# Where the query weights wait, and in what order the matrix engine takes expert rows and queries

## The reference

```python
def peer_ffn(h, w_q, sub_keys, expert_u, expert_v):     # 8 heads, 2 x 128 sub-keys, top 16
    q = einsum('cd,de->ce', xc, w_q)                     # (C, 8, 2, 128): 8 heads, 256 wide each
    s = einsum('chpk,pnk->chpn', q, sub_keys)
    sv, si = top_k(s, 16)                                # per half
    cand = sv[:, :, 0, :, None] + sv[:, :, 1, None, :]   # 256 candidates
    top_v, top_pos = top_k(cand, 16)
    gate = softmax(top_v)
    u = expert_u[eid]; act = gelu(einsum('cd,chkd->chk', xc, u))
    y = einsum('chk,chkd->cd', gate * act, expert_v[eid])
x = x + g2 * y
return rmsnorm(x, final_g)
```

## Time and profile before

| | |
|---|---|
| median of 3 executions | 1353.65 us (1345.6, 1353.65, 1353.81) |
| the profiled execution | 1349.08 us, of which the traced span 1347.3 us |
| mean granted PE clock | 0.939 |
| busy: PE, DVE, POOL, ACT | 85%, 67%, 33%, 19% |
| DMA | 412.99 MB, mean 307 GB/s |

### The profile page before, as it was taken

One profiled execution on the slowest core, in us unless ns is written; L12 is line 12 of the kernel. 1 busy time (PEld: TensorE's weight loads), 2 busy tenths in 40 slices (PEclk: granted clock), 3 DMA queues, 4 the chain that ended last, 5 costly groups with the idle time before them and its releaser, 6 DMA issues.

```text
span 1347.3 us, 13673 instructions
## 1 busy us (share of the span) xinstructions
PE 1147.1 (85%) x4566; PEld 756.0 (56%) x4566; DVE 903.4 (67%) x2164; ACT 258.0 (19%) x434; POOL 438.3 (33%) x351
## 2 busy tenths in 40 slices
PE   4899988986999996897999997778778787878876
PEld 3788877846999994864665653333323233323322
DVE  6453437535788886442577888696877869778565
ACT  2114022005333333432320101001010100101001
POOL 0000000012455541310134465444444444545430
PEclk9889999997999997898999999889999888998898
DMA  9546455543677664221399999999999999999992
GB/s 384 199 188 264 174 218 219 218 188 125 250 299 285 283 286 185 94 94 36 153 422 421 420 419 421 422 420 422 421 420 422 421 421 422 421 422 421 421 421 120
DMA packets 57220, 412.99 MB, mean 307 GB/s; under 512 B 6480, under 2 KB 6480, under 8 KB 7120
## 3 DMA queue, kind: packets, MB, share of 16 engines
q0 software_dynamic: 42912, 311.97, 56.3%
q1 hardware_dynamic: 14256, 100.37, 19.1%
HBM read 411.26 MB, written 1.05 MB: 306 GB/s over the span
## 4 chain that ended last, share of the span: by engine, by line
PE 54%; DMA 27%; DVE 12%; issue 4%; ACT 2%; POOL 1%; SPq 0%; DVEq 0%; ACTq 0%
PE ps L420 13%; PE ps L908 10%; DMA areaB<-in_experts,idx 7%; DMA gate_area<-in_experts,idx 7%; PE ps L433 6%; PE ps L435 6%; PE ps L434 5%; DMA ring<-in_experts,idx 4%; DMA mod_ring<-in_experts,idx 3%; DMA spare<-in_experts,idx 3%; PE ps L506 3%; PE ps L672 2%; DMA areaB<-in_mod_w 2%; PE ps L524 1%; DVE mod_sum L1833 1%
## 5 line engine op out<-in xcount | busy, mean ns | idle before, releaser
L908 PE MATMUL ps<-areaB,mod_sum 128*128 128x512 f32 x308 | 156.8, 652 | 38.6 <-DVE mod_sum L1833 38.5
L420 PE MATMUL ps<-hT,ring 128*128 128x256 f32 x832 | 187.3, 386 | 1.7 <-DMA ring<-in_stream 1.7
L420 PEld LDWEIGHTS ps<-hT,ring 128*128 128x128 f32 x832 | 160.3, 194 | 26.7 <-issue 2.6
L908 PE MATMUL ps<-gate_area,mod_sum 128*128 128x512 f32 x240 | 117.9, 640 | 32.0 <-DVE mod_sum L1833 32.0
L908 PEld LDWEIGHTS ps<-areaB,mod_sum 128*128 128x128 f32 x308 | 62.3, 207 | 125.9 <-issue 73.8
L1177 ACT ACTIVATE act<-now 128x2 f32<-128x2 f32 (+1 forms) x130 | 26.3, 203 | 553.3 <-DVE now L1824 553.2
L1269 POOL DMA_INDIRECT gate_area<-in_experts,idx x60 | 71.6, 1193 | 182.5 <-PE ps L908 90.4
L1824 DVE CUSTOM_DVE_ANT_0 areaB<-areaB,xn 128x1024 f32<-128x1024 f32 x77 | 93.4, 1223 | 48.4 <-DMA areaB<-in_experts,idx 48.3
L1269 POOL DMA_INDIRECT areaB<-in_experts,idx x77 | 94.1, 1222 | 94.1 <-PE ps L908 88.1
L433 PE MATMUL ps<-hT_h,w_lo 128*128 128x256 f32 x416 | 119.3, 287 | 3.8 <-DVE hT_l L1312 2.0
L1228 POOL TENSOR_TENSOR w_lo<-ring,w_hi 128x512 fp32r<-128x512 f32 x41 | 102.3, 2509 | 60.7 <-ACT w_hi L979 60.6
(11 more groups left out here) (312 smaller groups left out, 1873.5 us busy)
## 6 DMA issues: line engine op xcount, KB each, us to landing
ring<-in_stream SPq DMA_DIRECT2D x84, 1024.0 KB, 6.0
mod_ring<-in_mod_w POOLq DMA_DIRECT2D x40, 1024.0 KB, 6.8
gate_area<-in_mod_w SPq DMA_DIRECT2D x3, 1024.0 KB, 13.4
areaB<-in_mod_w SPq DMA_DIRECT2D x3, 1024.0 KB, 23.2
mod_ring<-in_mod_w SPq DMA_DIRECT2D x2, 1024.0 KB, 6.1
small<-in_small SPq DMA_DIRECT2D x1, 1352.0 KB, 28.4
areaB<-in_experts,idx POOLq DMA_INDIRECT x77, 23.3
x_sb<-in_x SPq DMA_DIRECT2D x1, 1024.0 KB, 9.2
```

Of the source, the lines that this page charges most:

```text
L420: last = mm(ps[:, bank, b * T:(b + 1) * T], w[:, at:at + P], rhs[:, k, :], start=(k == 0), stop=(k == KC - 1))
L908: last = mm(ps[:, B3 + 2 * t + b, :], spread_w[n // FEW % 2][:, n % FEW, :], row[ROW_OF[n]][:, D + 512 * b:D + 512 * b + 512], start=first ...
```

## The change

- All eight wq units get a place of their own: 0 to 2 in the ring slots, 3 in spare, 4 and 5 in mod_ring, 6 over constants that are no longer read (tile small), 7 in areaA. SP issues 3, 4 and 5 when the last unit that is split has been sent for, 6 and 7 behind wo2's last load, then 0, 1 and 2. None waits for an earlier query.
- Scores are kept in four places that come round, not eight, and the small arrays of the top-16 search move from mT into constants that are no longer read.
- The row places are now 7 at the start (gate_area, areaB), then the slot of wq 0 and mT: nine. Each further query frees a place (`ROW_JOINS`: row 9 takes that of wq 1, row 16 wq 2, 27, 40, 53, 66, 79 those of wq 3 to 7, row 80 hT), 17 in all. A row that joins waits for the end of its query.
- PE's order is a table: `ROWS_BEFORE_QUERY`.
- Rows pass singly: dot n, then the spread of n - 1; one gelu a row.
- The first half's norm, final scale and output are done between the last rows, and the last 128x512 piece is scaled by ACT and written from ACT's own DMA queue.

```diff
+EARLY_ROWS, ROWS = 9, 17
+ROWS_BEFORE_QUERY = {2: 6, 3: 16, 4: 28, 5: 40, 6: 52, 7: 64}
+ROW_JOINS = {9: (9, 1), 16: (10, 2), 27: (11, 3), 40: (12, 4), 53: (13, 5), 66: (14, 6), 79: (15, 7), 80: (16, 7)}
...
-            with sp.Fori(edge2, UNITS // RING) as i:
-                for s in range(RING):
-                    load(i, s, False)
+            load_query(3)
+            sp.wait_ge(mod_summed, MODS)
+            load_query(4)
+            load_query(5)
+            load(edge2, 0, False)
+            sp.wait_ge(pool_out, 1)
+            sp.wait_ge(at_p, 2)
+            load_query(6)
+            load_query(7)
...
+            load(edge2, 1, False)
+            load(edge2, 2, False)
+            load(edge2 + 1, 0, False)
...
             head_scores(1)
-            head_scores(2)
-            expert_sum(0)
-            head_scores(3)
-            for h in range(4, HEADS):
-                expert_sum(2 * h - 7)
-                expert_sum(2 * h - 6)
...
+            n = 0
+            for h in range(2, HEADS):
+                expert_sums(n, ROWS_BEFORE_QUERY[h])
+                n = ROWS_BEFORE_QUERY[h]
                 head_scores(h)
...
+            def gelu(n):
...
+                act.wait_ge(dot_done, n + 1)
+                A(act_now[n // FEW % 4][:, n % FEW:n % FEW + 1], now[n // FEW % 4][:, n % FEW:n % FEW + 1],
+                  ACT.Gelu).then_inc(gelu_done, 1)
...
+            gate_exp(0)
+            for n in range(EXPERTS_EACH):
+                gelu(n)
+                if n == 2:
+                    head_copy(1)
+                for h in range(2, HEADS):
+                    if n == ROWS_BEFORE_QUERY[h] + 2:
+                        head_copy(h)
...
+                if n in ROW_JOINS:
+                    pool.wait_ge(unit_done, DONE("wq", ROW_JOINS[n][1]))
+                if ROW_BEFORE[n] >= 0:
+                    pool.wait_ge(row_used, ROW_BEFORE[n] + 1)
...
+            for n in range(2, 8):
+                dot_product(n)
+                spread_weight(n - 1)
+                if n == 3:
+                    route_keys(0, 1)
+                if n == 5:
+                    route_pairs(0, 1)
+                    less_maximum(1)
+            spread(5, modT[:, 88:96])
...
-            for b in range(2):
-                half = slice(512 * b, 512 * b + 512)
-                V.scalar_tensor_tensor(out=xn[:, 1, half], in0=x_sb[:, 1, half], scalar=stat[:, 45:46],
-                                       in1=final_row[:, half], op0=ALU.mult, op1=ALU.mult).then_inc(out_ready, 1)
+            V.reciprocal(stat[:, 45:46], stat[:, 45:46]).then_inc(scale_out, 1)
+            dve.wait_ge(scale_out, 2)
+            V.scalar_tensor_tensor(out=xn[:, 1, 0:512], in0=x_sb[:, 1, 0:512], scalar=stat[:, 45:46],
+                                   in1=final_row[:, 0:512], op0=ALU.mult, op1=ALU.mult).then_inc(out_ready, 1)
...
+            act.wait_ge(scale_out, 2)
+            A(xn[:, 1, 512:], y_tmp[:, 0:512], ACT.Identity, scale=stat[:, 45:46]).then_inc(last_out, 1)
+            act.dma_start(out[P:2 * P, 512:], xn[:, 1, 512:]).then_inc(out_done, 16)
```

More of the change, by code:

```diff
@@ L11 @@
+from collections import deque
 from contextlib import ExitStack
@@ L72, in DONE @@
     return AT[kind, j] + 1
[L76 to L83, removed]
+ROW_OF, USE_OF, ROW_BEFORE = [], [], []
+_used = deque()
 for _n in range(EXPERTS_EACH):
-    if LATE_AT <= _n < LATE_AT + LATE_ROWS:
-        ROW_OF.append(EARLY_ROWS + _n - LATE_AT)
-    else:
[L88 to L95, removed]
+    if _n < EARLY_ROWS or _n in ROW_JOINS:
+        ROW_BEFORE.append(-1)
+        ROW_OF.append(_n if _n < EARLY_ROWS else ROW_JOINS[_n][0])
+    else:
+        ROW_BEFORE.append(_used.popleft())
+        ROW_OF.append(ROW_OF[ROW_BEFORE[_n]])
+    _used.append(_n)
+    USE_OF.append(ROW_OF.count(ROW_OF[_n]))
 HT_LAST = 16
@@ L236, in build @@
         pT = cut(areaB, 3072, 4, 384)
-        score = [cut(areaA, 4096 + 512 * h, 512) for h in range(HEADS)]
+        score = [cut(areaA, 4096 + 512 * (h % 4), 512) for h in range(HEADS)]
         y_tmp = cut(areaA, 4096, D)
@@ L264, in build @@
         w_in = [sem(f"w_in{s}") for s in range(RING)]
+        query_in = {h: sem(f"query_in{h}") for h in range(3, HEADS)}
         unit_done = sem("unit_done")
@@ L899, in head_scores, with expert_sums @@
                     sub_scores(h - 1)
[L901 to L904 removed]
+            def expert_sums(n0, n1):
+                for n in range(n0, n1):
+                    t = n // TOPK % NT
                     pe.wait_ge(spread_ready, n + 1)
@@ L1864, in _ @@
             dot_product(0)
-            spread(5, modT[:, 88:96])
             dot_product(1)
-            route_keys(0, 1)
-            dot_product(2)
-            dot_product(3)
             normalise_gates(0)
-            for n in range(FEW):
-                spread_weight(n)
-            for g in range(1, HEADS * GROUPS - 1):
-                h, k = g // GROUPS, g % GROUPS
-                for n in range(FEW * g, FEW * g + FEW):
-                    dot_product(n)
-                if g == 3:
-                    normalise_gates(1)
-                if h and k == 0:
-                    normalise_gates(h + 1)
-                for n in range(FEW * g, FEW * g + FEW):
-                    spread_weight(n)
-                if g == 1:
+            spread_weight(0)
@@ L1885, in _ @@
+            for n in range(2, 8):
[4 more added lines that the diff above has]
+                if n == 5:
                     route_pairs(0, 1)
                     less_maximum(1)
+            spread(5, modT[:, 88:96])
+            for n in range(8, EXPERTS_EACH):
+                g = n // FEW
+                h, k = g // GROUPS, g % GROUPS
+                dot_product(n)
+                spread_weight(n - 1)
+                if n == TOPK:
+                    normalise_gates(1)
+                elif n % (NT * TOPK) == 0:
+                    normalise_gates(h + 1)
+                if n == EXPERTS_EACH - 12:
+                    dve.wait_ge(row_ready, 12)
+                    dve.wait_ge(row_used, EXPERTS_EACH - TOPK)
+                    last_residual(0, 0)
+                    last_residual(0, 1)
+                if n == EXPERTS_EACH - 10:
+                    dve.wait_ge(sq_sum, 17)
+                    V.tensor_scalar(stat[:, 60:61], stat[:, 16:17], 1.0 / D, EPS, ALU.mult, ALU.add)\
+                        .then_inc(mean_sq, 1)
+                if n == EXPERTS_EACH - 8:
+                    dve.wait_ge(final_in, 16)
+                    dve.wait_ge(root, 8)
+                    step(V.reciprocal(stat[:, 44:45], stat[:, 44:45]))
+                    step.wait()
+                    V.scalar_tensor_tensor(out=xn[:, 0, :], in0=x_sb[:, 0, :], scalar=stat[:, 44:45], in1=final_row,
+                                           op0=ALU.mult, op1=ALU.mult).then_inc(out_ready, 1)
+                if n % FEW < FEW - 1:
+                    continue
```

118 lines of the change are left out of this document (48 added, 70 removed).

## The result

The changed kernel takes 1362.26 us (median of 6, 1357.41 to 1363.59), the kernel before 1348.62 us (median of 6, 1345.6 to 1353.81). The ratio is 1.009, 95% interval 1.007 to 1.011: slower by about 0.9%, little, but the interval lies above 1, where 1337 and a range of 1327 to 1347 were predicted. The profiled execution took 1357.41 us, its span is 1355.7 us, the mean granted PE clock 0.947.

A forecast was written before the change was run, and what follows sets the result against it. The prediction took DMA transfers, about 421 GB/s, to bound the kernel for 654 us. Its terms, -12.45 - 3.2 - 0.6 + 2.3 = -13.95 us, led to a forecast time of 1337 us, range 1327 to 1347.

The forecast's parts named there:

- (a): Full stretch of gathers: moving five query-weight units out of it saves 12.45 us, bounds 12.0 to 13.9.
- share below 0.9 up to row 60: Sign that the forecast is wrong: a DMA share under 0.9 in the stretch up to row 60.
- the units were not the cause: Rival, last landing: moved units did not delay it, one engine ends last; time 1347.6 us, chance 0.08.
- Row 23's dot: Sign that the forecast is right: this dot starts about 12 us nearer to the first gather's issue.
- (b): PE's tail, last landing to DVE's first use of the result: 3.2 us shorter, bounds 0.6 to 3.3.
- (c): Output at the end: ACT scales one piece beside DVE, saving 0.6 us, bounds 0 and 1.2.
- (d): Joins of rows 16, 27 and 40: waits for queries let DMA run dry, costing 2.3 us, bounds 0 to 5.
- The rival on the slow side: Rows passing singly make DVE the bound, each spread waiting for a gelu; time 1360 us, chance 0.06.
- dry for longer: Rival, first 60 rows: DVE is the bound, 8 us of DMA idle for 2.3; time 1340.8 us, chance 0.20.
- none: Rival, joins: no DMA dryness and the other terms at their better ends; time 1330.7 us, chance 0.10.

The follow-up runs named there:

- experiment 1: The changed kernel with the load of final_g and its wait for row_mm moved from gather 32 to gather 64; 1339.39 us, ratio 0.9944.
- experiment 9: The changed kernel, final_g still at gather 32, with both halves of the broadcast it waits for done in query 3; 1338.76 us, ratio 0.9939.
- experiment 8: experiment 6 with wq 3 to 7 sent for late again, each when the query three before is done; 1347.68 us, ratio 0.9991.
- experiment 6: experiment 1 with queries 2, 4 and 6 a row earlier on PE and rows 15, 39, 65 joining for 16, 40, 66; 1336.97 us, ratio 0.9913.
- experiment 2: experiment 1 with wq 3 to 7 sent for late again, each when the query three before is done; 1346.94 us, ratio 0.9996.
- experiment 4: experiment 1 with DVE doing four dots, then four spreads, from row 96 on, as before the change; 1341.3 us, ratio 0.9964.
- experiment 5: experiment 1 with SP holding the first half's 512 KB output until the last dot is done; 1339.82 us, ratio 0.9931.
- experiment 7: The edits of experiment 5 and experiment 6 together, final_g at gather 64; 1333.41 us, ratio 0.9891.

## Why the prediction was wrong

**The step that failed** is one sentence in (a): "final_g stays where it is". The load was costed at nothing because its lines don't change. But the wait ahead of it is on `row_mm`, which is raised by a broadcast inside query 4, and the change moves the end of query 4 from 726 to 767.6 us. The gathers stand behind the load in POOL's program, and none went out until the load had. It cost 19.2 us of stretch (experiment 1 against the changed kernel; 18.9 by experiment 9). By row 31 the changed kernel was well ahead: that row's weights land at 751.7 us (issue plus time to landing, 740.79 + 10.9) where before they landed at 763.3 (754.13 + 9.2), 11.6 sooner. Row 32's landed at 778.5 (770.11 + 8.4) against 767.0 (757.02 + 10.0), 11.5 later. The first gather was on time (666.13 against 666.40), and the hole is the "share below 0.9 up to row 60" that the prediction lists as a sign against it.

Everything that was needed to see it stood in the order of PE's instructions and the code: query 4 behind row 27, `broadcast_half` under `if h in (3, 4)`, and the wait for it in front of gather 32. Of a step that moves, all that it raises moves too; the prediction followed `unit_done`, which the joins wait for, and not `row_mm`. By its own numbers rows 0 to 31 are through at 666.4 + 4.3 + 32 x 2.49 = 750.4 us, so a gather 32 that is held far beyond that leaves the DMA with nothing to do.

**(a) Units out of the full stretch: right.** Forecast 12.45, bounds 12.0 to 13.9; measured 11.9 (experiment 8 against 6), just under the lower bound, and 8.3 where idle time hid a part (experiment 2 against 1). The rival that the units were not the cause falls with it. A unit costs 2.37 us, 95% of the 2.49 that its transfer takes. The bandwidth on which it rests was met again, 421 GB/s over 480 us. The Trainium skill, "DMA: Bandwidth & Descriptors", section "Where 436 GB/s comes from", has the HBM side bind at about 358 GB/s. No run here shows such a bound, but the kernel runs on one core, and no run here has a second core busy.

One sign was read from the wrong place. Row 23's dot was to come about 12 us nearer to the first issue; it starts at 737.54, 71.4 us after it, 5.3 nearer. Its row in the trace shows no wait for a landing, so DVE was behind its weights there, and the dot no longer tells when they landed.

**(b) PE's tail: right.** From the last landing to DVE's first use of the result are 1347.41 - 1342.98 = 4.43 us where 7.43 were the earlier trace rows; -3.0 against a forecast of -3.2. Experiment 4 puts up to 1.9 of it down to single rows. The rest was not tried, but the traces have a candidate, the granted clock. In the kernel before, with the clock at 0.50 from 1324 to 1328 us, PE's first two rows behind its wait at 1323.34 take 6.1 us. In experiment 4 PE's first two behind its last wait take 3.5, at a clock of 1.00. In the changed kernel it is 1.00 from 1334 to 1348 us. DVE kept up in spite of the norm between the last rows: rows 252 to 255 start on their landings.

Here ACT's table loads were weighed. The rows of ACT in the changed kernel, behind the square of the first half:

```profile
1320.17 1.28 ACT L1204 ACT_TABLE_LOAD   x1
1321.46 0.20 ACT L1204 ACTIVATE stat<-stat 128x1 f32<-128x1 f32 x1
1321.68 1.28 ACT L1187 ACT_TABLE_LOAD   x1
1322.98 0.30 ACT L1187 ACTIVATE act<-now 128x1 f32<-128x1 f32 x2
```

Root and gelu start 1.29 and 1.30 us after the loads began, so a change of table costs 1.3. The Trainium skill, "ScalarE: Activation LUTs", section "What ACT_TABLE_LOAD costs", adds 1.38 us of drain; neither of these two rows shows it.

**(c) The output: mis-sized.** Forecast -0.6, measured 0: from the first residual to the end are 1355.67 - 1347.41 = 8.26 us, before 8.24. The way to the first scaling is as long as it was (4.35 us, before 4.34), so DVE's product did lie beside ACT's square. The halves are scaled side by side and SP sends its piece 0.78 us after the scaling began, where before the second piece went out some 0.7 later. But the pieces land 2.6 and 2.7 us after their issue where they took 2.1, and from the first scaling to the end are 3.9 us in both. Why the pieces take longer is not shown.

**The first half's output: left out.** The forecast let it pass at no cost between the last rows. Its 512 KB took 7.8 us to land instead of 2.6, in a stretch where DMA is the bound, and the landings of two rows beside it came 1.2 us late in all (experiment 5). Held back, it gave 0.5 and 0.8 us of stretch (experiments 5 and 7), each within what single profiles scatter.

**(d) DMA dry at the joins: right mechanism, size within its bounds.** Experiment 1 has a stretch 7.6 shorter than before, where (a) measured 11.9. The missing 4.3 are 3.3 for the idle that experiment 6 takes away and 1.2 for the output, to within 0.2. So (d) measured 3.3; forecast 2.3, bounds 0 to 5. It showed about row 16 and row 40, as listed.

**The sum.** With the failed step set right, experiment 1 is the kernel that the prediction describes: 1339.39 against 1349.25, or 9.9 us gained by the medians and some 7.6 by the ratio, where 13.95 were forecast. By the profiles, with the moment of the first gather taken out, it is 7.6 + 3.0 = 10.6. The missing 3.35 are, to within 0.2, 1.2 for the output, 1.0 of (d), 0.6 of (c), 0.55 of (a) and 0.2 of (b). Its span of 1338.4 is 5.1 over the predicted 1333.3: these 3.35 and, but for rounding, a first gather that went out 1.6 later, at 667.99. Its median of 1339.4 lies inside the range.

**The rival on the slow side** had the sign and the wrong mechanism. Single passing costs no transfer. Among 185 spreads between 840 and 1300 us DVE waited 6 times for a gelu, 20.5 us in all, and the DMA stayed at 421 GB/s through it. Experiment 4 leaves the stretch as it is. For the rows ahead of its row 96, experiment 6 passes them singly too and keeps 417 to 427 GB/s in every window of 10 us from 680 to 860. The rival's 1360 us are near the measured 1362 by chance alone. The other rivals (dry for longer, none, units not the cause) describe kernels without the hole and were not what happened.

## What to carry to other kernels

Where an order table moves a step, list every semaphore that the step raises and everybody who waits on one, in lines that the diff doesn't touch above all; a wait in front of one DMA holds all that the same engine sends behind it, and in a stretch bound by DMA the time without a transfer is lost (19.0 us of missing transfer cost 19.2 here). A small load that nobody needs soon belongs well behind the step that it waits for. To price data taken out of a full stretch, first remove the idle time: the same five units measured 8.3 us with holes beside them and 11.9 without. And to see what a small transfer costs beside full ones, look at the distance between the landings next to it, which showed 1.2 us where the times showed nothing.

## What the hardware showed that was not expected

- A 512 KB output beside full gathers took 7.3 to 8.1 us to land (the changed kernel and experiments 1, 2, 4, 6, 8 and 9) where it takes 2.6 in a quiet stretch, and set the landings beside it back by 1.2 us in all.
- Two outputs of 256 KB from two queues land 2.6 and 2.7 us after their issue, two from one queue 2.1: the second queue gave no time here.
- In the profiles the first gather goes out between 664.9 and 670.3 us in kernels that compute the same up to there. A difference of spans below some 5 us needs its start taken out, as the stretches above do.
